# Two split weight buffers moved to other byte offsets in SBUF, in a float32 decoder layer

## The chip, the cores and the metric

The kernel runs on one core of a Trainium2 chip. The metric is the device time of one launch in microseconds (us), as the median of several runs. The profile is of one further execution; its times count from its first instruction.

## The reference

One decoder layer on 256 tokens of width 2048, all in float32. The weights make nearly all of the work:

```
h      = rms_norm(x)
proj   = h @ w_in                      # 2048 x 13312: q, k, v, gates of three branches
kv     = rms_norm(mem) @ w_mem_kv      # 2048 x 2048
o_da, o_ret, o_mem = differential attention, retention, attention into mem
merged = sum of sigmoid(gate_b) * (o_b @ w_o_b)       # three of 1024 x 2048
x      = x + merged @ w_out            # 2048 x 2048
hf     = rms_norm(x)
x      = x + (silu(hf @ w_gate) * (hf @ w_up)) @ w_down   # width 5632
```

## The kernel before, in words

**Tiles.** Every weight matrix is cut into "pairs": 256 rows by 512 columns, which lie in SBUF as [128 partitions, 2, 512] float32. There are 584 pairs. A pair is multiplied with both blocks of 128 tokens.

**Splitting.** To get float32 accuracy from the one-pass float32r format, each operand is split into a high part (the value rounded to float32r) and a low part (the value minus the high part). Three products are accumulated: high activation with high weight, high with low, low with high. The low with low product is left out. For one pair this makes 2 row halves x 2 token blocks x 3 products = 12 matmuls, in `three_passes` (lines 1007 to 1012):

```
for n, (a, w) in enumerate(((hi, w_hi), (hi, w_lo), (lo, w_hi))):
    e = pe.matmul(acc[p][:, t, :], a[:, k0 + k, tok], w[:, s % RING, k, :], ...)
```

The activation block (128x128) is the stationary operand, which TensorE loads ahead of each matmul. The weight row half (128x512) is the moving operand that streams past it.

**The ring.** The pairs go through three ring buffers of four slots each: `raw` (line 92), `w_hi` (93) and `w_lo` (94), 16384 bytes per partition each. A slot is 4096 bytes. For each pair:

- SyncE issues one DMA of 512 KB into a slot of `raw` (`load`, line 212). It waits until VectorE has finished with that slot four pairs earlier (`lo_done`).
- ScalarE copies the slot of `raw` to `w_hi` (`high`, line 337). It waits for the load and for the matmuls that used that slot of `w_hi` (`pair_used`).
- VectorE subtracts `w_hi` from `raw` and writes `w_lo` (`low`, line 625), after `hi_done`.
- TensorE waits for `lo_done` and runs the 12 matmuls (`pair`, line 1016).

The order of the work on every engine is written out by hand, pair by pair, and tied by counting semaphores; there is no planner. Between the pairs each engine does its share of the rest: TensorE does transposes against an identity (line 1032) and the small attention products (lines 1070, 1085 and others), which are plain float32 matmuls; ScalarE and VectorE do norms, softmax, gates, and the evacuation of PSUM (lines 365, 580, 585, 927, 951, 957 and others).

**Where the buffers lie.** `sb(name, shape, dtype)` takes the next piece of each SBUF partition, in the order of the program: `raw`, `w_hi`, `w_lo`, then the split activations `hT_hi`, `hT_lo`, `oT_hi`, `oT_lo` (16384 bytes each), then `proj`, `kvm`, `sq`, `qn`, `pm`, `ident`, `mask`, `rel`, and some small tensors. All of the buffers up to `rel` have a size that is a multiple of 512 bytes, so each begins at the same offset modulo 512 as the first one, called offset 0 here. A matmul's moving operand begins at a multiple of 2048 bytes in its buffer, and its stationary operand (one block of 128 tokens, 512 bytes) at a multiple of 512.

```
raw = sb("raw", [P, RING, 2, NCOL])
w_hi = sb("w_hi", [P, RING, 2, NCOL], F32R)
w_lo = sb("w_lo", [P, RING, 2, NCOL], F32R)
hT_hi = sb("hT_hi", [P, KD, TOK], F32R)
```

Of the kernel before, what the change touches and what calls it, by code (L numbers as in the profile page):

```python
# [33 lines left out]
P = 128  # L34
# [42 lines left out]
def program(nc, x, mem, positions, w_in, da_q_norm_g, da_k_norm_g, da_lambda_q1, da_lambda_k1,  # L77
# [6 lines left out]
    with ExitStack() as ctx:  # L84
        def sb(name, shape, dt=F32):
            return ctx.enter_context(nc.sbuf_tensor(name, shape, dt))
# [3 lines left out]


        raw = sb("raw", [P, RING, 2, NCOL])
        w_hi = sb("w_hi", [P, RING, 2, NCOL], F32R)
        w_lo = sb("w_lo", [P, RING, 2, NCOL], F32R)
        hT_hi = sb("hT_hi", [P, KD, TOK], F32R)
        hT_lo = sb("hT_lo", [P, KD, TOK], F32R)
        oT_hi = sb("oT_hi", [P, KD, TOK], F32R)
# [1181 lines left out]
```

## Time and profile before

| | |
|---|---|
| median of 3 runs | 1676.57 us (1676.52 to 1676.8) |
| span of the profiled execution | 1674.9 us |
| TensorE (PE) matmuls | 7592, busy 1668.0 us |
| VectorE (DVE) | busy 950.0 us |
| ScalarE (ACT) | busy 774.7 us |
| DMA | 319.96 MB, mean 191 GB/s |

The span runs from the first to the last instruction of the profiled execution. For that execution the profile gives no other time than this span, 1674.9 us, which is 1.67 us below the median of the runs. In the rows, L1010 is line 1010 of the kernel, "w_lo<-raw,w_hi" is what an instruction writes and reads, "128*128" is the part of the array that a matmul uses, and "x580" is a count. PE is the matmul, PEld the load of its stationary operand. Matmuls are pipelined, so the duration of one is longer than the distance from its start to the start of the next; this distance is called the spacing here.

### The profile page before, as it was taken

The numbers are of one execution on the slowest core, as the hardware profiler recorded it, in microseconds if no ns is written. First come the engines' busy times: TensorE is split into PE (matmuls) and PEld (weight loads), VectorE is DVE, ScalarE is ACT, GpSimd is POOL, SyncE is SP. The second block draws the span as 40 slices with busy tenths as digits, with TensorE's granted clock in tenths as the row PEclk, the third lists the DMA queues.
The fourth block names the chain that finished last, engine by engine and source line by source line (L and its number), as shares of the span: only waits on it lengthen the run. The fifth ranks groups of instructions, "written<-read, shape, count | busy, mean of one in ns | idle before, by whom it ended". The sixth has DMA issues, their size and how long they took to land.

```text
span 1674.9 us, 21891 instructions
## 1 busy us (share of the span) xinstructions
PE 1668.0 (100%) x7592; PEld 1381.3 (82%) x7592; DVE 950.0 (57%) x1061; ACT 774.7 (46%) x936; POOL 31.9 (2%) x33
## 2 busy tenths in 40 slices
PE   9999999999999999999999999999999999999999
PEld 7888888888888888888888888888888888888887
DVE  5565554454577766655555545565554554655555
ACT  6655454444555544444444544444434444444342
POOL 0000000000111000000000000000000000000000
PEclk9999999999999999999999999999999999999999
DMA  9876555566544565666655666666666666666664
GB/s 340 265 217 187 176 169 168 177 196 192 174 152 150 180 185 175 213 199 190 188 184 184 186 189 192 191 193 188 188 192 190 190 192 188 189 192 191 192 189 151
DMA packets 167095, 319.96 MB, mean 191 GB/s; under 512 B 11152, under 2 KB 15760, under 8 KB 166288
## 3 DMA queue, kind: packets, MB, share of 16 engines
q1 hardware_dynamic: 167056, 319.45, 62.1%
q8 instruction: 24, 0.39, 0.1%
q14 instruction: 15, 0.12, 0.0%
HBM read 317.31 MB, written 2.10 MB: 191 GB/s over the span
## 4 chain that ended last, share of the span: by engine, by line
PE 91%; issue 7%; DVE 1%; DMA 0%; POOL 0%; ACT 0%; DVEq 0%; ACTq 0%; SPq 0%; POOLq 0%
PE acc L1010 87%; PE at L1032 2%; POOL rstd L315 0%; PE at L1070 0%; PE at L1085 0%; DMA raw<-in_w_mem_kv 0%; DVE w_lo L625 0%; DMA raw<-in_w_in 0%; ACT pm L486 0%; PE at L1160 0%; DVE ss L650 0%; ACT w_hi L337 0%; PE at L1172 0%; PE at L1173 0%; PE at L1171 0%
## 5 line engine op out<-in xcount | busy, mean ns | idle before, releaser
L625 DVE TENSOR_TENSOR w_lo<-raw,w_hi 128x1024 fp32r<-128x1024 f32 x580 | 706.7, 1224 | 639.5 <-ACT w_hi L337 637.6
L337 ACT ACTIVATE w_hi<-raw 128x1024 fp32r<-128x1024 f32 x580 | 614.6, 1061 | 829.4 <-PE acc L1010 812.7
L1010 PE MATMUL acc<-w_hi,hT_hi 128*128 128x512 f32 x1568 | 616.7, 393 | 0.0
L1010 PE MATMUL acc<-w_hi,hT_lo 128*128 128x512 f32 x1568 | 611.0, 390 | 0.0
L1010 PE MATMUL acc<-w_lo,hT_hi 128*128 128x512 f32 x1568 | 610.5, 389 | 0.0
L1010 PEld LDWEIGHTS acc<-w_hi,hT_hi 128*128 128x128 f32 x1568 | 294.5, 188 | 62.2 <-issue 1.3
L1010 PEld LDWEIGHTS acc<-w_hi,hT_lo 128*128 128x128 f32 x1568 | 294.4, 188 | 61.9
L1010 PEld LDWEIGHTS acc<-w_lo,hT_hi 128*128 128x128 f32 x1568 | 294.6, 188 | 59.8
L1010 PE MATMUL acc<-w_hi,oT_hi 128*128 128x512 f32 x768 | 300.9, 392 | 1.2 <-DVE oT_lo L644 1.2
L1010 PE MATMUL acc<-w_hi,oT_lo 128*128 128x512 f32 x768 | 299.1, 389 | 0.0
L1010 PE MATMUL acc<-w_lo,oT_hi 128*128 128x512 f32 x768 | 299.0, 389 | 0.0
L1010 PEld LDWEIGHTS acc<-w_hi,oT_hi 128*128 128x128 f32 x768 | 144.2, 188 | 31.4 <-issue 1.6
L1010 PEld LDWEIGHTS acc<-w_hi,oT_lo 128*128 128x128 f32 x768 | 144.2, 188 | 30.1
L1010 PEld LDWEIGHTS acc<-w_lo,oT_hi 128*128 128x128 f32 x768 | 144.3, 188 | 29.4
L927 DVE TENSOR_TENSOR proj<-acc,proj 128x1024 f32<-128x1024 f32 x47 | 57.6, 1225 | 20.6 <-PE acc L1010 20.6
L315 POOL TENSOR_TENSOR rstd<-ms,minus_half 128x4 f32<-128x4 f32 (+1 forms) x16 | 26.9, 1680 | 613.4 <-DVE ms L651 613.4
L365 ACT ACTIVATE proj<-acc,row_rstd 128x512 f32 (+1 forms) x28 | 17.7, 685 | 23.6 <-PE acc L1010 23.6
L951 DVE SCALAR_TENSOR_TENSOR proj<-acc,row_rstd,proj 128x512 f32<-128x512 f32 x22 | 15.5, 747 | 5.9 <-PE acc L1010 5.9
L1032 PEld LDWEIGHTS at<-ident,proj 128*128 128x128 f32 x120 | 14.0, 140 | 2.0
L1032 PE MATMUL at<-ident,proj 128*128 128x128 f32 x120 | 15.5, 272 | 0.0
L650 DVE TENSOR_REDUCE ss<-sq 128x4 f32<-128x512 f32 (+2 forms) x16 | 15.1, 946 | 0.0
L472 ACT ACTIVATE proj<-acc,half_rstd 128x512 f32<-128x512 f32 x24 | 15.1, 681 | 0.0
(151 smaller groups left out, 474.9 us busy)
## 6 DMA issues: line engine op xcount, KB each, us to landing
raw<-in_w_in SPq DMA_DIRECT2D x208, 512.0 KB, 3.9
raw<-in_w_ffn_gate SPq DMA_DIRECT2D x88, 512.0 KB, 3.8
raw<-in_w_ffn_up SPq DMA_DIRECT2D x88, 512.0 KB, 3.7
raw<-in_w_ffn_down SPq DMA_DIRECT2D x88, 512.0 KB, 3.8
raw<-in_w_mem_kv SPq DMA_DIRECT2D x32, 512.0 KB, 6.5
raw<-in_w_out SPq DMA_DIRECT2D x32, 512.0 KB, 3.8
raw<-in_w_o_mem SPq DMA_DIRECT2D x16, 512.0 KB, 5.3
raw<-in_w_o_da SPq DMA_DIRECT2D x16, 512.0 KB, 5.0
```

Source lines behind the costliest of these rows:

```text
L315: nc.gpsimd.tensor_tensor(rstd[:, 0:n], ms[:, 0:n], minus_half[:, 0:n], ALU.pow).then_inc(done, 1)
L337: act.activation(w_hi[:, s % RING], raw[:, s % RING], ACT.Copy).then_inc(hi_done, 1)
L365: e = act.activation(dst[:, t], acc[p][:, t, :], ACT.Copy, scale=row_rstd[:, norm, t:t + 1])
L472: e = act.activation(sg[:, t], acc[0][:, t, :], ACT.Tanh, scale=half_rstd[:, t:t + 1])
L625: v.tensor_tensor(w_lo[:, s % RING], raw[:, s % RING], w_hi[:, s % RING].bitcast(F32), ALU.subtract).then_inc(lo_done, 1)
L650: step(v.tensor_reduce(ss[:, 0:n], src, AX.X, ALU.add), X[summed], i + 1)
L927: v.tensor_tensor(dst, acc[p][:], dst, ALU.add).then_inc(acc_free[p], 1)
L951: e = v.scalar_tensor_tensor(out=gt[:, t], in0=acc[1][:, t, :], scalar=row_rstd[:, 2, t:t + 1], in1=sg[:, t], op0=ALU.mult, op1=ALU.mult)
L1010: e = pe.matmul(acc[p][:, t, :], a[:, k0 + k, tok], w[:, s % RING, k, :], start=first and k == 0 and n == 0, stop=last and k == 1 and n == 2)
L1032: return pe.transpose(out, src, ident[:])
```

## The change

Three unused tensors are put beside the two split weight buffers. Before `w_hi` lie 48 floats (192 bytes) per partition, between `w_hi` and `w_lo` 40 floats (160 bytes), and after `w_lo` another 40. No instruction reads or writes them. `w_hi` then begins at 192 and `w_lo` at 192 + 160 = 352 bytes modulo 512. The three together take 512 bytes, so all that follows keeps its offset modulo 512.

```
         raw = sb("raw", [P, RING, 2, NCOL])
+        sb("before_hi", [P, 48])
         w_hi = sb("w_hi", [P, RING, 2, NCOL], F32R)
+        sb("before_lo", [P, 40])
         w_lo = sb("w_lo", [P, RING, 2, NCOL], F32R)
+        sb("after_lo", [P, 40])
         hT_hi = sb("hT_hi", [P, KD, TOK], F32R)
```

## Rows read from the trace of the kernel before

**Rows 1.** The page: busy time by engine, and the granted TensorE clock in 40 slices.

```profile
PE 1668.0 (100%) x7592; PEld 1381.3 (82%) x7592; DVE 950.0 (57%) x1061; ACT 774.7 (46%) x936; POOL 31.9 (2%) x33
DVE  5565554454577766655555545565554554655555
PEclk9999999999999999999999999999999999999999
```

**Rows 2.** The page: the chain that ended last, shares of the span by engine.

```profile
PE 91%; issue 7%; DVE 1%; DMA 0%; POOL 0%; ACT 0%; DVEq 0%; ACTq 0%; SPq 0%; POOLq 0%
```

**Rows 3.** The chain in order of time, 1050 to 1200: start us, us, what.

```profile
1061.97 65.33 PE acc L1010 x288
1127.30 0.88 PE at L1032 x8
1128.17 65.30 PE acc L1010 x288
```

**Rows 4.** Timeline of all engines from 1200: start us, us, instruction, idle before it.

```profile
1199.87 1.06 ACT L337 ACTIVATE w_hi<-raw 128x1024 fp32r<-128x1024 f32 x1 [1.66 <-PE acc L1010]
1200.13 0.39 PE L1010 MATMUL acc<-w_hi,hT_lo 128*128 128x512 f32 x1
1200.13 0.19 PEld L1010 LDWEIGHTS acc<-w_hi,hT_hi 128*128 128x128 f32 x1
1200.35 0.39 PE L1010 MATMUL acc<-w_hi,hT_hi 128*128 128x512 f32 x1
...
1200.96 1.23 DVE L625 TENSOR_TENSOR w_lo<-raw,w_hi 128x1024 fp32r<-128x1024 f32 x1 [1.49 <-ACT w_hi L337]
...
1202.85 0.39 PE L1010 MATMUL acc<-w_hi,hT_lo 128*128 128x512 f32 x1
```

**Rows 5.** Timeline of the matmuls alone, 221 to 224.6.

```profile
221.16 1.89 PE L1085 MATMUL at<-qn,pm 128*128 128x256 f32 x8
222.69 0.58 PE L1010 MATMUL acc<-w_hi,hT_hi 128*128 128x512 f32 x1
223.11 0.40 PE L1010 MATMUL acc<-w_lo,hT_hi 128*128 128x512 f32 x1
223.34 0.39 PE L1010 MATMUL acc<-w_hi,hT_lo 128*128 128x512 f32 x1
223.57 0.39 PE L1010 MATMUL acc<-w_hi,hT_hi 128*128 128x512 f32 x1
223.80 0.39 PE L1010 MATMUL acc<-w_lo,hT_hi 128*128 128x512 f32 x1
```

**Rows 6.** Instructions by line, shapes apart: busy us, mean ns, idle before and releaser.

```profile
L1010 PE MATMUL acc<-w_hi,hT_hi 128*128 128x512 f32 x1568 | 616.7, 393 | 0.0
L1010 PE MATMUL acc<-w_hi,oT_hi 128*128 128x512 f32 x768 | 300.9, 392 | 1.2 <-DVE oT_lo L644 1.2
L1085 PE MATMUL at<-qn,pm 128*128 128x256 f32 x32 | 7.5, 379 | 0.0
L337 ACT ACTIVATE w_hi<-raw 128x1024 fp32r<-128x1024 f32 x580 | 614.6, 1061 | 829.4 <-PE acc L1010 812.7 <-DMA raw<-in_w_in 13.0 <-DMA raw<-in_w_mem_kv 3.7
L625 DVE TENSOR_TENSOR w_lo<-raw,w_hi 128x1024 fp32r<-128x1024 f32 x580 | 706.7, 1224 | 639.5 <-ACT w_hi L337 637.6
L585 ACT ACTIVATE oT_hi<-at 128x1024 fp32r<-128x1024 f32 x10 | 10.1, 1010 | 0.0
L957 DVE TENSOR_TENSOR oT_lo<-at,oT_hi 128x1024 fp32r<-128x1024 f32 x10 | 12.2, 1218 | 0.0
```

**Rows 7.** Timeline of the matmuls alone, 14.2 to 17.6.

```profile
14.71 0.40 PE L1010 MATMUL acc<-w_lo,oT_hi 128*128 128x512 f32 x1
14.95 0.40 PE L1010 MATMUL acc<-w_hi,oT_lo 128*128 128x512 f32 x1
...
16.80 0.39 PE L1010 MATMUL acc<-w_lo,oT_hi 128*128 128x512 f32 x1
17.04 0.39 PE L1010 MATMUL acc<-w_hi,oT_lo 128*128 128x512 f32 x1
```

**Rows 8.** The page: DMA issues, count, KB each, median us to landing.

```profile
raw<-in_w_ffn_up SPq DMA_DIRECT2D x88, 512.0 KB, 3.7
```

More of the change, by code:

```diff
@@ L92, in program @@
         raw = sb("raw", [P, RING, 2, NCOL])
+        sb("before_hi", [P, 48])
         w_hi = sb("w_hi", [P, RING, 2, NCOL], F32R)
+        sb("before_lo", [P, 40])
         w_lo = sb("w_lo", [P, RING, 2, NCOL], F32R)
+        sb("after_lo", [P, 40])
         hT_hi = sb("hT_hi", [P, KD, TOK], F32R)
```

## The prediction, made before the change was built

> **What bounds the kernel now.** I read the page's busy table first. TensorE is busy for 1668.0 of 1674.9 us, at a granted clock of 9 tenths or more in every slice, the upper level of 2.4 GHz; VectorE is at 57% and ScalarE at 46% [rows 1]. A busy TensorE can still wait inside its pipeline, so the chain that ended last comes next: 91% of it is TensorE and 7% "issue", and DMA and ScalarE stand at 0% [rows 2]. In order of time it is one repeating piece, 288 matmuls in 65.33 us, 8 transposes in 0.88 us, and again [rows 3]. That is 24 pairs of 12 matmuls, the feed-forward part. So the time is the number of matmuls times their spacing, and the spacing is what an offset could change.
>
> **The spacing.** The starts of a matmul at 1200.13 and of the one twelve later at 1202.85 are 2.72 us apart, 226.7 ns each [rows 4]; 65.33 us for 288 gives 226.8 with the restart after the transposes [rows 3]. At 2.4 GHz 512 columns take 512 / 2.4 = 213.3 ns, so each matmul has 13.3 ns that are not columns. In the six groups of line 1010 there are 3 x 1568 + 3 x 768 = 7008 such matmuls (the first group of each kind stands in [rows 6]). 7008 x 226.7 ns = 1588.7 us. What is left, 1674.9 - 1588.7 = 86.2 us, is the other 584 matmuls, the start, the end and short restarts. The span is 1.67 us below the median of the runs, 1676.57, and I carry every difference over to that median.
>
> **The change part by part.** It adds no instruction, DMA or wait and takes none away. It moves two buffers. These are the accesses that get another offset:
>
> 1. *TensorE reads the moving operand* from `w_hi` (two passes of three) at 192 and from `w_lo` (one of three) at 352 modulo 512, instead of 0. The activations stay at 0. The trace has no matmul whose operand starts elsewhere, since all large buffers begin at 0 modulo 512, so this cost must be bounded. From below: the matmuls of line 1085 have 256 columns, float32. The profile has two records for each call, and eight records take 1.89 us [rows 5]. With 379 ns for the last [rows 6], (1.89 - 0.38) / 7 = 215.7 ns. That is the best spacing of a long matmul here, also with a stationary load for each. If the shift brought 226.7 down to it, the gain is 11.0 ns x 7008 = 77.1 us; with nothing left but columns it is 13.3 x 7008 = 93.2 us. From above: ten spacings from 14.71 to 17.04 us are 233.0 ns [rows 7], the slowest continuous stream that I find, 6.3 ns more. On the w_lo passes alone (7008 / 3 = 2336) that is +14.7 us, on all +44.2 us. I take 0. The reason is how uniform the spacing is. It is 0.22 to 0.23 us while ScalarE writes `w_hi` (from 1199.87), while VectorE reads `raw` and `w_hi` and writes `w_lo` (from 1200.96), and when neither runs [rows 4]; the mean is 389 to 393 ns per record whether the activations come from `hT` or `oT` [rows 6]. A stream that other accesses to SBUF do not disturb is nearest to one that a new start does not disturb either.
>
> 2. *ScalarE writes `w_hi`, VectorE reads it and writes `w_lo`* at the new offsets. Now they take 1061 and 1224 ns. The nearest rows of the same size with other sources are 1010 and 1218 ns [rows 6], the lower bounds. For the upper one I take twice the time, as nothing excludes it. At today's times the cover is wide: VectorE has a slot ready at 1200.96 + 1.23 = 1202.19, and TensorE comes to it three pairs after 1199.87, at 1199.87 + 3 x 2.72 = 1208.03 [rows 4]. That leaves 5.8 us, and ScalarE idles 829.4 us, 812.7 of them waiting for TensorE; VectorE idles 639.5 us [rows 6]. So up to some 1.2 us more for each costs nothing on the average. Doubled, VectorE would be busy 950.0 + 706.7 = 1656.7 us, which still fits, but not in the three slices in which it is at 7 tenths [rows 1]: there 41.9 us x 0.75 + 15.4 x 1.22 = 50.2, about 8 us too much in each, 25 us in all. I take 0.
>
> 3. *The load of `raw`.* `raw` itself stays. SyncE issues the next load when VectorE is done, 1202.19, it lands 3.7 us later [rows 8], at 1205.9, and ScalarE wants it at 1199.87 + 4 x 2.72 = 1210.8. Cost 0, with 4.9 us of cover, and if w_lo were written later the load would move by as much.
>
> 4. *Everything behind.* All buffers after `w_lo` move by 512 bytes and keep their offset modulo 512. Cost 0.
>
> Sum: 0 + 0 + 0 + 0, so 1676.6 us.
>
> **What the Trainium skill says.** The row shows a stationary load (PEld) starting in the same hundredth of a microsecond as each matmul, so two streams are read from SBUF at once [rows 4]. The Trainium skill, "SBUF — State Buffer", section "Who interferes with whom", gives TensorE two independent read ports, one for the moving operand and one for the load, and says that TensorE and ScalarE never wait on anyone. By that rule the sum is 0 whatever the offsets. The trace agrees in that no other engine's work shows in the spacing; it can't show the part about the two reads, since in it they always overlap. Against this stands the size of the spacing. The Trainium skill, "TensorE: Matmul & The Clock Gate", section "Back-to-back issue gap", gives N/2.4 + 2.5 ns, 215.8 ns for 512 columns. The measured 226.7 ns differs and decides. By the page something takes 10.9 ns from every matmul here, which as an estimate from that page would be 76 us for 7008 of them.
>
> **The rivals.**
>
> *A. The two reads collide when both start at 0 modulo 512, and the shift parts them.* For it: the excess of 13.3 ns is seen only where the moving operand is read at full rate, 2048 bytes per partition in 226.7 ns. The 256-column records read half of that or less in 215.7 ns and have 2.4 ns of excess, with the same load beside them [rows 5, 6]. Each load reads 512 bytes that begin at the same place modulo 512 as the row that streams beside it. Against it: the spacing right after a restart, where load and matmul lie otherwise, is no better (starts at 223.11, 223.34, 223.57 and 223.80 [rows 5]) and never falls below 226 over any long piece [rows 3]; a cost fixed by the float32r format itself, or by the switch to the new stationary block, explains it just as well. Price: 77.1 us as above, 1676.6 - 77.1 = 1599.5 us.
>
> *B. Starts off a round boundary cost.* This one ends slower. 352 is not a multiple of 64 where 192 is, so a row of `w_lo` would touch one piece of memory more than now, at every w_lo pass, on TensorE's own path with nothing to hide it. Price: the w_lo passes at the 233.0 ns of the start-up stretch [rows 7], 14.7 us, so 1691.3 us; if 192 is no round offset either, all passes, 44.2 us, 1720.8 us. It decides from 1.4 ns on a w_lo pass (3.35 / 2336), or 0.5 ns on every pass. For it: the spacing is exposed in full. Against it: no row shows any sensitivity to an address.
>
> *C. The unused tensors do not shift anything,* because they are placed elsewhere or the sizes are rounded up. The time is then 1676.6 us again, and the profile cannot tell it from my forecast.
>
> **How the numbers follow.** A measurement of this kernel can tell about 0.2%, 3.35 us, from no change. The forecast and C together are "within 0.2%": 0.72, since every cost but one is hidden and the one exposed is uniform across all that varies in the trace. A, or a part of its gain, has 0.17: the unexplained 11 ns is real, but its cause is open, and that it hangs on the start modulo 512 is one of several readings. B in its forms has 0.11, of which 0.09 lies at or below 1691.3 us. The likeliest is 1676.6 us. The range takes in the unchanged case and the nearer form of B, from 1676.6 - 3.35 = 1673.2 to 1692 us, 0.72 + 0.09 = 0.81; left out are A and the dear form of B, 0.19.
>
> **What would show it right or wrong.** Right: twelve matmuls of line 1010 still take 2.72 us, 288 of them 65.3 us, w_hi 1061 ns and w_lo 1224 ns. A is right if the pair takes about 12 x 215.7 = 2.59 us, with ScalarE waiting less for TensorE. B is right if the spacing after a w_lo matmul is longer than after the two w_hi ones. If the ScalarE or VectorE durations change while the pair stays at 2.72 us, point 2 is wrong in size and right in its cover. The forecast falls if the spacing moves by over 0.5 ns.

## The result and the profile after

The changed kernel takes 1706.53 us (median of 4 runs, 1705.79 to 1707.12), the kernel before 1676.68 us in the same comparison: +29.9 us, a ratio of 1.0176 with a 95% interval from 1.0164 to 1.0188. The prediction was no change, 1676.6 us, with a range up to 1692 us. The change made the kernel slower, and the time lies above the range.

The page of the changed kernel, the busy table and the clock, which answer to [rows 1]:

```profile
PE 1696.4 (100%) x7592; PEld 1380.6 (81%) x7592; DVE 950.6 (56%) x1061; ACT 775.1 (45%) x936; POOL 28.8 (2%) x33
PEclk9999999999999999999999999999999999999999
```

The counts are the same, the clock too, and VectorE and ScalarE are as busy as before to within 0.6 us. Only TensorE is busy for longer, by 28.4 us. The instructions by line, of the changed kernel (line 1010 is now 1013, 625 is 628, 337 is 340), which answer to [rows 6]:

```profile
L628 DVE TENSOR_TENSOR w_lo<-raw,w_hi 128x1024 fp32r<-128x1024 f32 x580 | 706.9, 1224 | 668.3 <-ACT w_hi L340 665.7
L340 ACT ACTIVATE w_hi<-raw 128x1024 fp32r<-128x1024 f32 x580 | 615.1, 1061 | 858.0 <-PE acc L1013 845.7
L1013 PE MATMUL acc<-w_hi,hT_hi 128*128 128x512 f32 x1568 | 621.7, 396 | 0.0
L1013 PEld LDWEIGHTS acc<-w_hi,hT_hi 128*128 128x128 f32 x1568 | 294.1, 188 | 69.6 <-issue 1.3
```

VectorE's 1224 ns and ScalarE's 1061 ns have not moved, though both now work on buffers at other offsets; they wait longer, ScalarE 845.7 us for TensorE instead of 812.7. So the new time is in the matmuls. The chain in order of time, of the changed kernel (start us, us, what), which answers to [rows 3]; the second line is from the projections and branches further ahead:

```profile
1079.91 66.57 PE acc L1013 x288
1146.48 0.87 PE at L1035 x8
```
```profile
724.78 110.37 PE acc L1013 x473
```

288 matmuls take 66.57 us where they took 65.33: 231.1 instead of 226.8 ns each. The transposes take 0.87 us as before. In the second stretch it is 110.37 / 473 = 233.3 ns, with the same offsets modulo 512 and the same sizes. The timeline of the matmuls, of the changed kernel, shows how the 231.1 are made up, against the even steps of [rows 4]:

```profile
1202.66 0.40 PE L1013 MATMUL acc<-w_hi,oT_hi 128*128 128x512 f32 x1
1202.90 0.39 PE L1013 MATMUL acc<-w_lo,oT_hi 128*128 128x512 f32 x1
1203.13 0.39 PE L1013 MATMUL acc<-w_hi,oT_lo 128*128 128x512 f32 x1
1203.36 0.39 PE L1013 MATMUL acc<-w_hi,oT_hi 128*128 128x512 f32 x1
1203.59 0.39 PE L1013 MATMUL acc<-w_lo,oT_hi 128*128 128x512 f32 x1
1203.82 0.39 PE L1013 MATMUL acc<-w_hi,oT_lo 128*128 128x512 f32 x1
1204.05 0.40 PE L1013 MATMUL acc<-w_hi,oT_hi 128*128 128x512 f32 x1
```

Six starts are 1204.05 - 1202.66 = 1.39 us apart, 231.7 ns each at this resolution. At the trace's own resolution of 1 ns the six steps are 235, 232, 229, 226, 233 and 232 ns, and then again 235: a pattern that repeats with the six matmuls of one weight row half. Before, the first steps after each restart were uneven, and every step after the tenth, 6096 in all, was 225 to 228 ns. In the changed kernel no stretch has even six such steps in a row. The mean step is longer whatever streams: 232.5 ns from the start of a `w_lo` matmul to the next start, and 230.7 and 231.1 ns from the two `w_hi` ones.

The sum over the trace: the 6858 distances under 245 ns between one matmul of this kind and the next have a mean of 231.4 ns and make 1587.1 us; before there were 6856 with 227.0 ns, 1556.4 us. That is 30.7 us more. All other distances between matmuls, the restarts among them, make 1.3 us less, so 29.4 us remain, and the span grew by 1704.4 - 1674.9 = 29.5 us.

### The profile page after: what moved, and what is told of

Read it like the earlier page. It is cut to its first block, busy times and chain, and to the rows that moved or that the text cites. A ratio compares the mean times of both kernels' runs of the same rounds, so it can differ in the third digit from the quotient of the medians.

```text
span 1704.4 us, 21891 instructions
## 1 busy us (share of the span) xinstructions
PE 1696.4 (100%) x7592; PEld 1380.6 (81%) x7592; DVE 950.6 (56%) x1061; ACT 775.1 (45%) x936; POOL 28.8 (2%) x33
## 4 chain that ended last, share of the span: by engine, by line
PE 99%; DMA 0%; DVE 0%; SPq 0%; ACT 0%; issue 0%
PE acc L1013 95%; PE at L1035 2%; PE at L1073 0%; PE at L1088 0%; DMA raw<-in_w_mem_kv 0%; PE at L1124 0%; PE at L1122 0%; PE at L1163 0%; PE at L1176 0%; PE at L1175 0%; PE at L1140 0%; PE at L1139 0%; PE at L1138 0%; PE at L1174 0%; DVE w_lo L661 0%; ACT w_hi L377 0%
## 5 line engine op out<-in xcount | busy, mean ns | idle before, releaser
L628 DVE TENSOR_TENSOR w_lo<-raw,w_hi 128x1024 fp32r<-128x1024 f32 x580 | 706.9, 1224 | 668.3 <-ACT w_hi L340 665.7
L340 ACT ACTIVATE w_hi<-raw 128x1024 fp32r<-128x1024 f32 x580 | 615.1, 1061 | 858.0 <-PE acc L1013 845.7
L1013 PE MATMUL acc<-w_lo,hT_hi 128*128 128x512 f32 x1568 | 617.5, 394 | 0.0
```

Of the source, the lines that this page charges most:

```text
L340: act.activation(w_hi[:, s % RING], raw[:, s % RING], ACT.Copy).then_inc(hi_done, 1)
L628: v.tensor_tensor(w_lo[:, s % RING], raw[:, s % RING], w_hi[:, s % RING].bitcast(F32), ALU.subtract).then_inc(lo_done, 1)
```

## The experiments

**What the distance is between.** The first four take the change apart: one buffer alone, the other alone, the activations in their place, and everything together. The letters of the theories here aren't those of the rivals in the prediction; only theory B is the same idea as rival B. After the result, theory R said that the distance between the moving operand and the stationary one loaded beside it counts; theory A, the start of the moving operand by itself; theory B, only starts that are no multiple of 64 bytes; theory C, ScalarE's and VectorE's accesses.

*w_hi alone at 192.*

```
+        sb("before_w_hi", [P, 48])
         w_hi = sb("w_hi", [P, RING, 2, NCOL], F32R)
+        sb("before_w_lo", [P, 80])
         w_lo = sb("w_lo", [P, RING, 2, NCOL], F32R)
```

> Only w_hi moves, to 192 bytes modulo 512; w_lo and all that follows go back to 0. The changed kernel was 29.9 us slower, and its spacing rose from 226.7 to about 231.1 ns on passes of both buffers. Theory R (what counts is the distance modulo 512 between the moving operand and the stationary one that is loaded beside it): two passes of three are moved, so about two thirds of it, +20 us, about 1696 us. Theory A (what counts is where the moving operand begins by itself): the same here, +20 us. Theory B (only the start that is no multiple of 64 bytes, that of w_lo, costs): 1676.6 us, no change. Theory C (ScalarE's and VectorE's accesses to w_hi collide with TensorE's reads): some loss, and more spacing only in the stretches in which they run.

Measured: 1726.73 us, ratio 1.030 (1.027 to 1.033), +50.1 us. R and A, with +20 us, missed the size (C named none): moving one of the two buffers costs more than moving both. B, with no change, is out. The chain, 288 matmuls of the feed-forward part, 234.5 ns each:

```profile
1091.59 67.53 PE acc L1012 x288
```

*w_lo alone at 352.*

```
+        sb("before_w_lo", [P, 88])
         w_lo = sb("w_lo", [P, RING, 2, NCOL], F32R)
+        sb("before_hT_hi", [P, 40])
```

> Only w_lo moves, to 352 bytes modulo 512; w_hi stays at 0, and what follows w_lo goes back to 0. Theories R and A: one pass of three is moved, about a third of the 29.9 us, +10 us, 1686.6 us. Theory B (only a start that is no multiple of 64 bytes costs): all of it, 1706 us, unless the loss lay in how the passes follow one another.

Measured: 1704.66 us, ratio 1.0168 (1.0138 to 1.0197), +28.0 us. R and A, with +10 us, missed again. B's 1706 us was near, but w_hi alone had already ruled out its mechanism. The chain of this kernel, 231.1 ns per matmul, as in the changed kernel:

```profile
1079.12 66.56 PE acc L1012 x288
```

Moving one pass of three costs nearly what moving all three does, so the passes don't each pay for themselves. The median steps are 233 ns (while `w_hi` streams), 231 (`w_lo`) and 229 (`w_hi` again), so the two passes that have not moved at all are slow as well.

*The activations moved, the weights left.*

```
+        sb("before_hT_hi", [P, 80])
         hT_hi = sb("hT_hi", [P, KD, TOK], F32R)
...
+        sb("before_proj", [P, 48])
         proj = sb("proj", [P, TB, GATE0])
```

> raw, w_hi and w_lo stay where they are; the four activation buffers hT and oT move to 320 bytes modulo 512, so that the weights lie 192 bytes behind them modulo 512, as w_hi in the changed kernel; what follows goes back to 0. Theory R: all three passes are moved in distance, +25 to +35 us, about 1706 us. Theory A: the moving operands begin where they did, 1676.6 us, no change. Theory B: 320 is a multiple of 64, no change.

Measured: 1719.79 us, ratio 1.0258 (1.0228 to 1.0288), +43.1 us. Theories A and B said no change; A is out too. R had the direction, with +25 to +35 us too little. The timeline of the matmuls of this kernel:

```profile
1200.20 0.39 PE L1012 MATMUL acc<-w_hi,oT_lo 128*128 128x512 f32 x1
1200.43 0.40 PE L1012 MATMUL acc<-w_hi,oT_hi 128*128 128x512 f32 x1
1200.67 0.39 PE L1012 MATMUL acc<-w_lo,oT_hi 128*128 128x512 f32 x1
1200.90 0.40 PE L1012 MATMUL acc<-w_hi,oT_lo 128*128 128x512 f32 x1
1201.14 0.39 PE L1012 MATMUL acc<-w_hi,oT_hi 128*128 128x512 f32 x1
```

The steps alternate, 0.23, 0.24, 0.23, 0.24 us (231 and 236 ns), whatever the pass: another offset gives another rhythm.

*Everything moved by 192.*

```
+        sb("before_raw", [P, 48])
         raw = sb("raw", [P, RING, 2, NCOL])
```

> 192 unused bytes ahead of raw, so that every buffer of the kernel moves by 192 bytes and all distances stay. Theory R: no change, 1676.6 us, spacing 226.7 ns. Theory A: every moving operand begins 192 bytes later modulo 512, +30 us or so, 1706 us. Theory B: 192 is a multiple of 64, no change.

Measured: 1677.37 us, ratio 1.0003 (0.9991 to 1.0014). No change, as theory R said (and B, which was out by then). The chain of this kernel:

```profile
1062.23 65.30 PE acc L1011 x288
1127.54 0.87 PE at L1033 x8
1128.41 65.33 PE acc L1011 x288
```

With all distances kept, 192 bytes do nothing. It is distances that count: moving the stationary operands against the moving ones (the run before) costs 43.1 us, moving both together nothing.

**Which distances are good.** Five kernels give each ring slot an offset of its own, so that one trace shows four offsets: s1, s2, s3 and s5 move w_hi and w_lo alike, s4 moves w_lo alone. The edit, for s1:

```
-        w_hi = sb("w_hi", [P, RING, 2, NCOL], F32R)
+        w_hi = []
+        sb("pad_w_hi0", [P, 8])
+        w_hi.append(sb("w_hi0", [P, 2, NCOL], F32R))
+        sb("pad_w_hi1", [P, 8])
+        w_hi.append(sb("w_hi1", [P, 2, NCOL], F32R))
...
-    e = pe.matmul(acc[p][:, t, :], a[:, k0 + k, tok], w[:, s % RING, k, :],
+    e = pe.matmul(acc[p][:, t, :], a[:, k0 + k, tok], w[s % RING][:, k, :],
```

> Each of the four ring slots is a tensor of its own and begins at another offset, the same for w_hi and w_lo: slot 0 at 32, slot 1 at 64, slot 2 at 128, slot 3 at 256 bytes modulo 512; the activations stay at 0. The mean spacing over the 12 matmuls of a pair is read for each slot. Theory R, that the distance to the stationary operand counts: each slot has a spacing of its own, 226.7 to 236 ns; if the loss is in crossings from one piece of memory to the next, multiples of some size (64, 128 or 256) stay at 226.7. A rival (R-any): every distance but 0 costs the same, 231 to 233.3 ns, as 192 did when the activations were moved (233.3 ns). Another (R-gain): some distance comes out below 226.7 ns, down to the 215.7 ns of the 256-column matmuls.

> The same with the slots at 16, 96, 160 and 384 bytes modulo 512. Theory R: as above; 384 lies 128 before the activations, so it is as 128 if only the size of the distance counts. R-any: 231 to 233.3 ns on all four. R-gain: one of them under 226.7 ns.

> The same with the slots at 192, 224, 448 and 480 bytes modulo 512. Slot 0 repeats the distance of 192 with both weight buffers, as when the activations were moved: theory R gives 233.3 ns. 448 and 480 are -64 and -32; if the sign does not count they are as 64 and 32.

> The slots of w_hi stay at 0, those of w_lo lie at 32, 64, 128 and 256 bytes modulo 512. If only the distance of each moving operand to the activations counts, the excess over 226.7 ns of each slot is one third of that of the slot with the same offset in s1. If instead the distance between the moving operands of successive matmuls counts (w_hi alone at 192 cost more, 234.4 ns, than both moved, 231.1), it is larger than a third, up to more than the whole.

> Slots of w_hi and w_lo at 8, 240, 272 and 320 bytes modulo 512, activations at 0. It asks how sharp the good points at 0 and 256 are. If only distances of exactly a multiple of 256 keep the 226.7 ns, all four are at 229 to 234 ns. If a few bytes are let pass, 8, 240 and 272 stay near 227 ns. A slot under 226.7 ns would be a better layout than that of before.

Measured times: s1 1701.01, s2 1709.93, s3 1716.31, s4 1703.02, s5 1719.22 us (one run each, against 1676.5 and 1677.15 us). The spacing by slot, worked out from the start times in each trace as the mean of the twelve distances from one start to the next, over the 105 to 117 pairs of the slot with nothing else on TensorE between them:

```
w_hi and w_lo, bytes modulo 512   mean spacing, ns
   0 (before)                     226.7
   8 (s5)                         234.0
  16 (s2)                         233.2
  32 (s1)                         233.6
  64 (s1)                         229.8
  96 (s2)                         231.4
 128 (s1)                         231.8
 160 (s2)                         230.3
 192 (s3)                         233.7
 224 (s3)                         232.9
 240 (s5)                         235.5
 256 (s1)                         227.2
 272 (s5)                         232.9
 320 (s5)                         231.4
 384 (s2)                         233.3
 448 (s3)                         232.6
 480 (s3)                         232.6
w_hi at 0, w_lo at 32 / 64 / 128 / 256 (s4)   231.7 / 231.3 / 232.6 / 228.3
```

The timeline of s1 shows the slots at 128 and 256 follow one another; a pair begins at 1353.40, at 1356.18 and at 1358.90:

```profile
1353.40 0.39 PE L1028 MATMUL acc<-w_hi,hT_hi 128*128 128x512 f32 x1
...
1355.94 0.40 PE L1028 MATMUL acc<-w_hi,hT_lo 128*128 128x512 f32 x1
1356.18 0.39 PE L1028 MATMUL acc<-w_hi,hT_hi 128*128 128x512 f32 x1
1356.41 0.39 PE L1028 MATMUL acc<-w_lo,hT_hi 128*128 128x512 f32 x1
1356.63 0.39 PE L1028 MATMUL acc<-w_hi,hT_lo 128*128 128x512 f32 x1
...
1358.90 0.40 PE L1028 MATMUL acc<-w_hi,hT_hi 128*128 128x512 f32 x1
```

The pair at 128 takes 2.78 us, the one at 256 takes 2.72 us, as in [rows 4]. Of seventeen offsets only 0 and 256 keep the 226.7 ns (the 227.2 is one slow step at the border of two slots and eleven of 227); 8 bytes off zero lose it, and so do 16 bytes to either side of 256. The loss does not grow with the distance, and the sign does not mirror (32 and 480, 128 and 384, 64 and 448 differ by 1.0, 1.5 and 2.8 ns). Differences of that size are to be read with care, since each slot begins in the rhythm of the slot before, and no other order of the slots was run. That 256 is free and the others are not does not hang on this: the slot at 256 in s1 is at 226 to 227 ns from its second step on, and that in s4 from its fifth (the four before are 236, 228, 233 and 231 ns, which make the 228.3), while no other displaced slot comes to rest there in its twelve steps. 192 repeats the 233.3 ns of the moved activations, which lie at the same distance modulo 512, within 0.4 ns. No offset comes out under 226.7 ns, so R-gain fails, and R-any too, since 256 is free. In s4 the third of each excess that theory R in its simple form wanted, 1 to 2.3 ns, came out as 4.6 to 5.9 ns for 32, 64 and 128.

*w_hi alone again, but at 256.*

```
+        sb("before_w_hi", [P, 64])
         w_hi = sb("w_hi", [P, RING, 2, NCOL], F32R)
+        sb("before_w_lo", [P, 64])
         w_lo = sb("w_lo", [P, RING, 2, NCOL], F32R)
```

> w_hi begins at 256 bytes modulo 512, w_lo at 0 again. In s1 the slot at 256 came to 226.7 ns after the first four matmuls and in s4 that with w_lo at 256 to 227 ns, while 16 to 224 and 384 to 480 gave 229.8 to 233.8. If distances count modulo 256, this kernel has none, neither to the activations nor between w_hi and w_lo: 226.7 ns, 1676.6 us, no change. If they count modulo 512, it is slower by 10 us or more.

Measured: 1676.66 us, ratio 1.0001 (0.9990 to 1.0012). The chain of this kernel, beside that of w_hi at 192 (67.53 us), shows that a distance of 256 is as good as 0:

```profile
1061.64 65.33 PE acc L1012 x288
1126.96 0.87 PE at L1034 x8
1127.84 65.30 PE acc L1012 x288
```

Whether every other distance also repeats after 256 bytes isn't shown: in the slots 16 and 272 differ by 0.3 ns, but 64 and 320 by 1.6 and 128 and 384 by 1.5, behind different slots.

**Load or stream, and who else.** Three questions were left: does a stationary operand matter where no moving one has moved, have ScalarE and VectorE a part in it, and what does the size of the two reads do.

*Only the low activations moved, to 192.*

```
         hT_hi = sb("hT_hi", [P, KD, TOK], F32R)
+        sb("before_hT_lo", [P, 48])
         hT_lo = sb("hT_lo", [P, KD, TOK], F32R)
+        sb("before_oT_hi", [P, 80])
         oT_hi = sb("oT_hi", [P, KD, TOK], F32R)
+        sb("before_oT_lo", [P, 48])
         oT_lo = sb("oT_lo", [P, KD, TOK], F32R)
+        sb("before_proj", [P, 80])
```

> raw, w_hi and w_lo stay; of the activations only the low parts, hT_lo and oT_lo, move to 192 bytes modulo 512. Every moving operand begins where it did, and two of three stationary ones too. If the distance between load and stream counts and the spacing depends on the whole sequence, as the cut kernels suggest, all three passes lose the 226.7 ns, not only the third: mean 230 to 235 ns, 1700 to 1730 us. If each pass pays for its own distance, a third of the 6.7 ns that all activations at 320 cost: about 228.9 ns, 1692 us. If only moving operands count: no change.

Measured: 1703.57 us, ratio 1.0156 (1.0126 to 1.0185), +26.4 us. The chain of this kernel, 231.1 ns per matmul:

```profile
1077.50 66.56 PE acc L1014 x288
```

No moving operand lies elsewhere than before, and of the loads only each third one. So where the moving operands begin relative to one another can't be what counts here, and in the run with all activations moved the loads kept their distances among themselves and it was slow. What the two have in common is another distance between load and stream. The loss is in the whole sequence: the mean steps of the three passes are 229.8, 230.6 and 232.9 ns.

*Only raw moved, to 192.*

```
+        sb("before_raw", [P, 48])
         raw = sb("raw", [P, RING, 2, NCOL])
+        sb("before_w_hi", [P, 80])
         w_hi = sb("w_hi", [P, RING, 2, NCOL], F32R)
```

> Only raw moves, to 192 bytes modulo 512. It is read by ScalarE and VectorE and written by DMA, never by TensorE, and lies at another distance to w_hi and w_lo, as in the changed kernel. If the loss is TensorE's own two reads: no change, 1676.6 us, 226.7 ns. If ScalarE's or VectorE's accesses at another distance have a part in it: slower, or their own 1061 and 1224 ns change.

Measured: 1676.91 us, ratio 0.9999 (0.9988 to 1.0010). The chain and the two conversions of this kernel take what they took:

```profile
1061.95 65.33 PE acc L1012 x288
```
```profile
L627 DVE TENSOR_TENSOR w_lo<-raw,w_hi 128x1024 fp32r<-128x1024 f32 x580 | 706.4, 1224 | 639.6 <-ACT w_hi L339 637.6
L339 ACT ACTIVATE w_hi<-raw 128x1024 fp32r<-128x1024 f32 x580 | 614.7, 1061 | 828.2 <-PE acc L1012 809.7 <-DMA raw<-in_w_in 12.8 <-DMA raw<-in_w_mem_kv 5.7
```

The distance from `raw` to the split buffers has no part in the loss. That leaves theory C without support; a conflict of the writes to `w_hi` and `w_lo` with TensorE's reads of the activations has no run of its own, but the trace with the activations moved speaks against it: its 1020 steps under 245 ns in which neither buffer is being written have a mean of 233.8 ns, the 4263 with a write all through 233.3 ns.

*A smaller load in the middle pass, in both layouts.*

```
-                tok = slice(t * P, (t + 1) * P)
                 for n, (a, w) in enumerate(((hi, w_hi), (hi, w_lo), (lo, w_hi))):
-                    e = pe.matmul(acc[p][:, t, :], a[:, k0 + k, tok], ...
+                    m = (64, 32)[k] if n == 1 else P
+                    tok = slice(t * P, t * P + m)
+                    e = pe.matmul(acc[p][0:m, t, :], a[:, k0 + k, tok], ...
```

> The layout of before. In the middle pass of the three (high activation with w_lo) the stationary operand has 64 columns in the first row half and 32 in the second, instead of 128, so the product with w_lo is left out for the other tokens of each block. It tests what the 13.3 ns over the 213.3 ns of 512 columns belong to. If the load's own read of SBUF takes them from the stream (theory R, by its amount), the spacing from the first pass to the middle one falls from 226.7 to about 220 ns with 64 columns and 216.7 ns with 32, about 11 to 13 us less in all. If they are fixed for a pass, nothing changes, 1676.6 us.

> The same cut of the stationary operand in the layout of the changed kernel (w_hi at 192, w_lo at 352). If the extra 4.4 ns come from the load's read meeting the stream, a smaller read meets it less often: the mean spacing falls by more than in the layout of before, and the time comes out below 1706.5 us by more than e5_half does below 1676.6 us. If they come from the moving operand alone, the difference of the two layouts stays at 29.9 us.

Measured, one run each: 1695.39 us in the layout of before, 18.5 us *slower* than the 1676.9 us of before in the same comparison, with less work; and 1704.14 us in the layout of the changed kernel, 2.4 us under 1706.53. The loads of the first one, from its timeline:

```profile
1200.96 0.14 PEld L1011 LDWEIGHTS acc<-w_lo,hT_hi 128*64 128x64 f32 x1
1201.19 0.19 PEld L1011 LDWEIGHTS acc<-w_hi,hT_lo 128*128 128x128 f32 x1
1201.42 0.19 PEld L1011 LDWEIGHTS acc<-w_hi,hT_hi 128*128 128x128 f32 x1
1201.65 0.11 PEld L1011 LDWEIGHTS acc<-w_lo,hT_hi 128*32 128x32 f32 x1
```

The loads are shorter, 0.14 and 0.11 us instead of 0.19, yet 288 matmuls take longer than the 65.33 us of before, 229.8 ns each:

```profile
1072.72 66.17 PE acc L1011 x288
```

Neither outcome expected for this kernel came: the first was a gain, the second no change. All offsets are as before; what differs is that successive loads are no longer alike. The edit also narrows the output in PSUM to 64 or 32 partitions in that pass, and which of the two counts was not tried. In the changed layout, where the even rhythm was lost already, the same cut leaves the feed-forward part as it was (66.57 us for 288). So the spacing did not fall there as the load reading wanted, nor did the difference of 29.9 us stay; it shrank to 8.8 us.

*Fewer columns in the middle pass, the layout of before.*

```
+                    c = (384, 256)[k] if n == 1 else NCOL
-                    e = pe.matmul(acc[p][:, t, :], a[:, k0 + k, tok], w[:, s % RING, k, :],
+                    e = pe.matmul(acc[p][:, t, 0:c], a[:, k0 + k, tok], w[:, s % RING, k, 0:c],
```

> The layout of before. In the middle pass the moving operand has 384 columns in the first row half and 256 in the second, instead of 512; the product with w_lo is left out for the other columns. If the excess of 13.3 ns belongs to each load, whatever streams beside it, the spacing of that pass is 160.0 + 13.3 = 173.3 ns and 106.7 + 13.3 = 120.0 ns. If it belongs to the columns that stream (13.3 ns for 512), it is 170.0 and 113.3 ns.

Measured: 1531.03 us. The timeline of the matmuls of this kernel:

```profile
1200.33 0.34 PE L1011 MATMUL acc<-w_lo,oT_hi 128*128 128x384 f32 x1
1200.51 0.40 PE L1011 MATMUL acc<-w_hi,oT_lo 128*128 128x512 f32 x1
1200.74 0.40 PE L1011 MATMUL acc<-w_hi,oT_hi 128*128 128x512 f32 x1
1200.98 0.27 PE L1011 MATMUL acc<-w_lo,oT_hi 128*128 128x256 f32 x1
1201.09 0.40 PE L1011 MATMUL acc<-w_hi,oT_lo 128*128 128x512 f32 x1
1201.32 0.39 PE L1011 MATMUL acc<-w_hi,oT_hi 128*128 128x512 f32 x1
```

The question it was made for stays open: the steps of 384 columns are 168 to 180 ns and those of 256 are 112 to 125, too uneven to tell 173.3 from 170.0 or 120.0 from 113.3 ns. But the passes with all 512 columns, which were not touched, now take 228 to 236 ns, 233.2 in the mean. Again the even 226.7 ns are gone as soon as the sequence is uneven.

**What follows.** The spacing of 226.7 ns is a rhythm of loads and streams, not a sum of a fixed cost per operand. It was found only where the starts of TensorE's operands are equal modulo 256 bytes and all sizes of the sequence are equal. In every other layout or sequence the 512-column steps have means from 229.8 to 235.5 ns. That the distance decides is shown; by what mechanism the load holds the stream up is not. None of the fifteen kernels that were run does the whole work faster than the kernel before, so there is no better version to show; three layouts (everything moved, w_hi at 256, raw alone at 192) equal it.

## Why the prediction was wrong, point by point

*What bounds the kernel* was right. TensorE's chain of 7008 matmuls times their spacing is the time, and the loss is spacing: 30.7 us more, less 1.3 us elsewhere.

*Point 1, the moving operand, is the step that failed.* The bounds, -13.3 to +6.3 ns, held for the changed kernel (+4.4 ns), though w_hi alone (+7.7 ns, 234.4) and the slots at 240 (+8.8 ns) lie outside them. The value taken, 0, rested on this: "A stream that other accesses to SBUF do not disturb is nearest to one that a new start does not disturb either." The rows did show that other engines don't disturb TensorE, and `raw` at another distance confirms it. They could say nothing about TensorE's own load, which overlaps every stream, at the same distance modulo 512 every time. An even spacing in a trace in which all offsets are equal is no evidence that offsets don't matter; it was the equality that made it even. The upper bound, the start-up stretch at 233.0 ns [rows 7], was about the right size: a stretch that hasn't settled yet runs in the kernel before at what the displaced layouts keep for good. The lower bound was weaker than it looked. It sets a float32 record of 256 columns beside 512 columns of float32r; 256 / 2.4 is 106.7 ns, so the 2.4 ns of excess are there only if a float32 column counts for two, which no run tried.

*Points 2, 3 and 4* were right. 1061 and 1224 ns did not change, the load of `raw` was not late, and moving everything behind by 512 bytes cost nothing (w_hi at 256 moves it by as much).

*Rival A* had the right pair, the load and the stream beside it, and the wrong sign. It read the excess of 13.3 ns over the columns as the collision of equal offsets. Of seventeen offsets none went under 226.7 ns, so that excess is not to be had this way; what it consists of is not known.

*Rival B* had the right sign. Charging the w_lo passes alone it came to 1691.3 us; w_lo alone measured 1704.7. Its mechanism is out: w_hi at 192, a multiple of 64, costs +50.1 us, and everything moved by 192 costs nothing. The sign by which it was to be known, a longer spacing after a w_lo matmul, did appear (232.5 ns against 230.7 and 231.1), so that sign could not tell it from a loss of the whole sequence. Its dear form, 1720.8 us, was above the result, and the range ended at 1692 us, between the two forms and below the result, because I gave 0.09 of B's 0.11 to the cheap form, which charged each pass on its own. Two passes that never moved slowed with the third.

*Rival C* is out: the unused tensors did shift the buffers, since the spacing moved by 4.4 ns.

*The rule of the Trainium skill,* "SBUF — State Buffer", section "Who interferes with whom", that TensorE's two read ports are independent and that TensorE never waits on anyone, gave 0. For the other engines this case agrees (raw alone at 192: ratio 0.9999). For TensorE's own two reads the measurements differ and decide: with nothing but each third stationary operand moved by 192 bytes, the stream slows by 4.4 ns a matmul. *"TensorE: Matmul & The Clock Gate"* of the Trainium skill, section "Back-to-back issue gap", has no offset in its 215.8 ns, which it calls the gap of an isolated matmul; for a stream of loads and matmuls it gives about 131 ns at 512 columns. Neither is what the traces show, 226.7 ns at best and 235.5 at worst for the same 512 columns.

## What to carry to other kernels

Keep the stationary and the moving operands of a dense stream of float32r matmuls at equal starts modulo 256 bytes (0 and 256 are the good distances found), and check it again when a small tensor is allocated between them: 8 bytes were enough to cost 7 ns of 227, and 192 bytes ahead of one buffer cost 3% of this kernel. Compare the spacing from start to start, not the duration of a record, and try a displaced layout on the chip before reading an even spacing as indifference. A resource that is always used in the same way in a trace shows no variation and so gives no evidence on what variation would cost.

## What the runs showed of the hardware

- The spacing of 512-column float32r matmuls, each with its own load of 128 columns, was 226.7 ns with all starts equal modulo 256 bytes (offsets 0 and 256 of 512), and 229.8 to 235.5 ns at fifteen other offsets. At 2.4 GHz 226.7 ns are 544 cycles, 32 more than columns.
- The loss belongs to the sequence. The changed kernel has two patterns with the same offsets and sizes, 231.1 ns and, from 724.78 to 835.15 us, 233.3 ns. Its trace shows them change at restarts: the first steps after the restart at 845.01 us are 320, 231, 235 and 234 ns and the 233.3 stay, those after the one at 865.49 us are 320, 235, 231 and 236 ns and the 231.1 are back. So how the stream is entered seems to count as well; no run set it on purpose.
- Less work can be slower: cutting the stationary operand of each third matmul from 128 to 64 or 32 columns, and its output with it, cost 18.5 us (one run).
- The float32 matmuls with 256 columns take 1.89 us for eight records in the changed kernel too, as in [rows 5], and the transposes 0.87 us for eight. They were not displaced in it, so whether they are as sensitive was not tried.
- How the memory behind this is organized, and why 32 cycles remain at the best offsets, these runs don't show.
